# Rows for a decoder trunk's second norm: transposes of y, partly ahead of the up projection, and x added per token

## What is computed

```python
y = jnp.concatenate([o_da, o_gla], axis=-1) @ w_out[l]
h_res = h_res + rmsnorm(y, post_mix_g[l])
h = rmsnorm(h_res, pre_ffn_g[l])
y = conv_ffn(h, w_up[l], conv_w[l], conv_b[l], w_down[l])
h_res = h_res + rmsnorm(y, post_ffn_g[l])
```

## Time and profile before

| | us |
|---|---|
| Median of three runs | 1216.88 |
| Lowest and highest | 1216.7, 1217.07 |
| Profiled execution | 1216.32 |
| Its span | 1214.5 |
| Busy: PE, DVE, ACT, POOL | 1201.5, 663.1, 604.6, 479.8 |

### The profile page before, as it was taken

The page is one execution under the profiler, slowest core; times in us unless marked ns, Lnnn a source line. Parts: engine busy times, 40 slices in busy tenths (PEclk is TensorE's granted clock), DMA queues, the critical chain, the costliest instruction groups (busy, mean ns, idle before and its releaser), DMA issues.

```text
span 1214.5 us, 23728 instructions
## 1 busy us (share of the span) xinstructions
PE 1201.5 (99%) x8948; PEld 1143.9 (94%) x8948; DVE 663.1 (55%) x963; ACT 604.6 (50%) x906; POOL 479.8 (40%) x221
## 2 busy tenths in 40 slices
PE   9999999999999999999999999999999999999997
PEld 8999999999999999999999999999999988888885
DVE  7765545554564346766666666666656743232234
ACT  7544445455674447544445445444444544444444
POOL 1233333323424433444444444444444444444443
PEclk9999999999999999999999999999999999999999
DMA  9655554544436645556565565565655565655641
GB/s 344 188 162 152 150 163 140 146 134 130 148 124 203 192 158 167 171 183 189 174 189 175 176 186 176 186 190 169 193 178 169 192 202 186 198 191 189 200 163 70
DMA packets 172751, 212.31 MB, mean 175 GB/s; under 512 B 6688, under 2 KB 158624, under 8 KB 172576
## 3 DMA queue, kind: packets, MB, share of 16 engines
q1 hardware_dynamic: 172272, 210.32, 55.9%
q10 hardware_dynamic: 432, 1.34, 0.3%
HBM read 209.53 MB, written 2.10 MB: 174 GB/s over the span
## 4 chain that ended last, share of the span: by engine, by line
PE 93%; DVE 3%; ACT 2%; issue 1%; DMA 1%; SPq 0%; DVEq 0%; ACTq 0%
PE psum L416 68%; PE psum L1779 19%; PE psum L1649 1%; PE psum L1419 1%; DVE a_lo L1249 1%; DVE w_lo L400 1%; ACT w_hi L396 1%; DMA raw<-in_w_first 1%; PE psum L1479 1%; PE psum L1807 0%; PE psum L1505 0%; DVE psum L1257 0%; DVE xT L1265 0%; PE psum L1588 0%; PE psum L1606 0%
## 5 line engine op out<-in xcount | busy, mean ns | idle before, releaser
L400 POOL TENSOR_TENSOR w_lo<-raw,w_hi 128x1024 fp32r<-128x1024 f32 x188 | 464.2, 2469 | 707.2 <-ACT w_hi L396 707.2
L416 PE MATMUL psum<-a_hi,w_hi 128*128 128x258 f32 (+1 forms) x2360 | 675.0, 286 | 0.9 <-ACT temp L596 0.8
L416 PE MATMUL psum<-a_lo,w_hi 128*128 128x258 f32 (+1 forms) x2360 | 673.8, 286 | 0.0
L416 PE MATMUL psum<-a_hi,w_lo 128*128 128x258 f32 (+1 forms) x2360 | 670.1, 284 | 0.0
L396 ACT ACTIVATE w_hi<-raw 128x1024 fp32r<-128x1024 f32 x391 | 411.4, 1059 | 470.7 <-PE psum L416 341.5
L400 DVE TENSOR_TENSOR w_lo<-raw,w_hi 128x1024 fp32r<-128x1024 f32 x204 | 269.0, 1320 | 412.0 <-ACT w_hi L396 411.0
L416 PEld LDWEIGHTS psum<-a_hi,w_hi 128*128 128x128 f32 x2360 | 448.3, 190 | 6.6 <-issue 4.3
L416 PEld LDWEIGHTS psum<-a_lo,w_hi 128*128 128x128 f32 x2360 | 448.5, 190 | 0.0
L416 PEld LDWEIGHTS psum<-a_hi,w_lo 128*128 128x128 f32 x2360 | 446.1, 189 | 0.1
L1309 DVE SCALAR_TENSOR_TENSOR proj<-proj,par 128x256 f32<-128x256 f32 x88 | 111.6, 1269 | 38.3 <-ACT proj L812 38.3
L1779 PE MATMUL psum<-w_hi,a_lo 128*128 128x512 f32 x336 | 130.7, 389 | 0.0
(11 more groups left out here) (234 smaller groups left out, 607.8 us busy)
## 6 DMA issues: line engine op xcount, KB each, us to landing
raw<-in_w_up SPq DMA_DIRECT2D x176, 512.0 KB, 3.6
raw<-in_w_in SPq DMA_DIRECT2D x88, 512.0 KB, 4.1
raw<-in_w_down SPq DMA_DIRECT2D x88, 512.0 KB, 4.0
raw<-in_w_out SPq DMA_DIRECT2D x32, 512.0 KB, 3.6
raw<-in_w_first SPq DMA_DIRECT2D x7, 512.0 KB, 10.4
xT<-in_features SPq DMA_DIRECT2D x3, 544.0 KB, 7.2
temp<-in_post_ffn_g ACTq DMA_DIRECT2D x1, 1024.0 KB, 4.7
out<-proj SPq DMA_DIRECT2D x2, 512.0 KB, 2.7
```

The source lines that it names most:

```text
L400: eng.tensor_tensor(w_lo[:, j % SPLIT, :], raw[:, j, :], w_hi[:, j % SPLIT, :], ALU.subtract)\
L416: mm = pe.matmul(psum[:, bank + m, 0:t1 - t0], w[:, j % SPLIT, cols], a[:, k, t0:t1], start=(k == 0 and step == 0), stop=(k == KT - 1 and ...
```

## The change

The transposes for the rows with tokens on partitions are now those of y (`y_T`), not of the sum. They need nothing of the first norm, so groups 0 to 3 stand ahead of the up projection, in banks 5, 0, 1 and 7 and in place of the eight products of constants; the up projection waits until groups 0 to 2 have been copied, VectorE's scaling until group 0 has been. Groups 4 to 7 follow chunks 2 to 5. ScalarE only copies a group. What was missing in it is made per token: x in its natural form (`x_nat`, two loads of 128x2048 on ScalarE's queue from a new input) is added on VectorE, four times 128x1024 (`add_rows`: y times its factor, plus x), and ScalarE squares each result with a sum (`natural_square`). The tokens are grouped so that the first norm's factors lie by token as well: two halo tokens apart, then 2 x 128.

Orders changed with it: ScalarE's split of chunk 3 and the load of the last gain go behind the second scaled tile; VectorE splits chunk 2 right behind the reciprocal, and chunk 3, which was GpSimd's, where it split chunk 2; its first `up_lo` goes ahead of the scaling of tiles 2 and 3; the second norm's row is spread behind chunk 10, not 9, and the splits of chunk 12 go behind the roots and the reciprocals.

The core of the diff:

```diff
-        GROUPS = ((0, P), (P, 2 * P), (NQ - P, NQ))
+        GROUPS = (NM, NM + P, 0)
         SUMS = 260
-        def nat_bank(n):
-            return ROW_BANK if n == 7 else NAT_BANK
+        NAT_BANKS = (Y2_BANK + 1, 0, 1, NAT_BANK, NAT_BANK, NAT_BANK, NAT_BANK, NAT_BANK)
...
+            def load_rows(t):
+                act_e.dma_start(x_nat[:, t, :], x_rows[t * P:(t + 1) * P, :]).then_inc(x_nat_landed, 16)
...
+            def natural(n):
+                act_e.wait_ge(nat_full, n + 1)
+                copy(x1_nat[:, n % 2, (n // 2) * BANK:(n // 2 + 1) * BANK], psum[:, NAT_BANKS[n], :]).then_inc(nat_free, 1)
+
+            def natural_square(t, h):
+                act_e.wait_ge(nat_added, 2 * h + t + 1)
+                act_e.activation(x_nat[:, t, h * CHUNK:(h + 1) * CHUNK], x1_nat[:, t, h * CHUNK:(h + 1) * CHUNK], ACT.Square,
+                                 accum_out=x1_ss[:, t, h:h + 1]).then_inc(nat_squared, 1)
...
+            dve.wait_ge(nat_free, 1)
             for k in range(2):
                 scale_y(k, k + 1, k + 1)
                 add_x(k, k + 1, k + 1)
             for g in range(1, KT // 2):
+                if g == 1:
+                    up_lo(0)
                 scale_y(2 * g, 2 * g + 2, g + 2)
-                up_lo(2 * g - 2)
+                if g > 1:
+                    up_lo(2 * g - 2)
                 add_x(2 * g, 2 * g + 2, g + 2)
                 up_lo(2 * g - 1)
                 if g == 2:
-                    split_lo(dve, OUT1 // RAW, 2)
+                    dve.wait_ge(lo_ready_p, (OUT1 + 2) // 2)
+                    split_lo(dve, OUT1 // RAW, 3)
...
+            def add_rows(t, h):
+                dve.wait_ge(nat_free, 4 * h + 4)
+                dve.wait_ge(x_nat_landed, 32)
+                x1 = x1_nat[:, t, h * CHUNK:(h + 1) * CHUNK]
+                dve.scalar_tensor_tensor(out=x1, in0=x1, scalar=y_rstd[:, t:t + 1],
+                                         in1=x_nat[:, t, h * CHUNK:(h + 1) * CHUNK], op0=ALU.mult, op1=ALU.add)\
+                    .then_inc(nat_added, 1)
...
-            busy(Y2_BANK, 2)
+            natural(0)
+            natural(1, 0, 2)
             pe.wait_ge(y_rstd_made, 1)
...
-            busy(NAT_BANK, 6)
+            natural(1, 2, 4)
+            natural(2)
+            natural(3)
...
             pe.wait_ge(tiles_evacuated, N_BEFORE_UP)
+            pe.wait_ge(nat_free, 3)
...
-                natural(j - 1)
-            natural(7)
-            pe.wait_ge(nat_free, 7)
+                if j < 6:
+                    pe.wait_ge(nat_free, j + 2)
+                    natural(j + 2)
+            pe.wait_ge(nat_free, 8)
```

More of the change, by code:

```diff
@@ L574, in _ @@
                         split_lo(pool, i + (IN1 + j + STREAM_LEAD) // RAW, (j + STREAM_LEAD) % RAW)
+            for c in range(OUT1 - RAW + STREAM_LEAD, OUT1 + STREAM_LEAD - 2):
+                if not lo_on_vector(c):
+                    split_lo(pool, c // RAW, c % RAW)
+            pool.wait_ge(lo_ready_p, (OUT1 + STREAM_LEAD) // 2)
             with pool.Fori(0, N_UP) as i:
@@ L772, in _ @@
                 out_half(i, 1)
+            load_rows(1)
             out_half(N_OUT - 1, 0)
@@ L840, in _ @@
             split_ahead_up(0, 0)
[L841 to L845, removed]
+            for k in range(6, 10):
+                up_hi(k)
             split_ahead_up(0, 1)
-            natural(1)
+            natural(4)
             up_hi(10)
@@ L1434, in spread @@
                 rows = rstd.shape[0]
-                last = cols.stop - cols.start
-                return pe.matmul(psum[:, bank, cols], rstd.broadcast_to([rows, P]), ident[0:rows, rows - last:rows],
+                return pe.matmul(psum[:, bank, cols], rstd.broadcast_to([rows, P]), ident[0:rows, 0:cols.stop - cols.start],
                                  start=True, stop=True)
@@ L1696, in token_sums, with natural @@
             def token_sums(n, squares):
-                for c, (a, b) in enumerate(GROUPS):
-                    mm = pe.matmul(psum[:, ROW_BANK, SUMS + c:SUMS + c + 1], squares[:, a:b], ones[:, 0:1],
-                                   start=(n == 0 and c == 0), stop=(n == 1 and c == 2))
-                return mm
+                for c in (2, 0, 1):
+                    rows = NM if n == 1 and c == 2 else P
+                    a = GROUPS[c]
+                    mm = pe.matmul(psum[0:rows, ROW_BANK, SUMS + c:SUMS + c + 1], squares[:, a:a + rows], ones[:, 0:1],
+                                   start=(n == 0 and c == 2), stop=(n == 1 and c == 1))
+                return mm
+            def natural(n, a=0, b=4):
+                t0 = NM + (n % 2) * P
+                mm = transposes(NAT_BANKS[n], [(kk * P, y_T[:, 4 * (n // 2) + kk, t0:t0 + P]) for kk in range(a, b)])
+                if b == 4:
+                    mm.then_inc(nat_full, 1)
+            for kk in range(4):
+                mm = product(2, RAW - 1, kk, 0, KT - 4 + kk, NQ)
+            mm.then_inc(y_half_made, 1)
+            for kk in range(4):
+                mm = product(3, RAW - 1, kk, 1, KT - 4 + kk, NQ)
+            mm.then_inc(chunk_used, 1)
             pe.wait_ge(y_summed, 2 + KT // 2)
@@ L1718, in up_chunk @@
                 project_chunk(pe, i + OUT1 // RAW, j, bank or 2 * (j // 4), 0, NQ)
[L1720 to L1724, removed]
-                transposes(nat_bank(n), [(kk * P, xT[:, 4 * (n // 2) + kk, t0:t0 + P]) for kk in range(4)])\
-                    .then_inc(nat_full, 1)
             pe.wait_ge(tiles_evacuated, N_BEFORE_UP)
+            pe.wait_ge(nat_free, 3)
             for j in range(2):
```

66 lines of the change are left out of this document (34 added, 32 removed).

## The result

| | before | after |
|---|---|---|
| Median, us | 1217.13 | 1219.20 |
| Profiled execution | 1216.32 | 1218.96 |
| Its span | 1214.5 | 1217.2 |
| Chunk 0 starts | 449.62 | 449.94 |
| Up projection ends | 966.44 | 969.23 |

The changed kernel takes 1.0018 times as long, with a 95% interval of 1.0012 to 1.0025. That is 2.07 us, just inside the 0.2% (2.4 us) that the prediction called the least that can be told from no change, and on the slow side of it. 1219.9 had been forecast. In the profiled executions the difference is 2.64 us. The medians of before and after are those of their common comparison, 19 executions of each.

A forecast was written before the change was run, and what follows sets the result against it. It took TensorE's issue times to bound the kernel. Terms -2.74 + 0.6 + 0.1 + 0.8 + 1.15 + 1.8 + 1.3 gave +3.0 us, 1219.3 for the profiled execution, and with 0.56 for the median 1219.9; range 1214.5 to 1221.3.

The forecast's parts named there:

- The likeliest case: GpSimd first at chunk 5, first add held, two late holds: 1219.9 us, range 1218.7 to 1220.9, chance 0.50.
- Part 1: Transposes ahead of the up projection: chunk 0 0.2 to 0.3 us late but hidden, gross gain 2.74 us by chunk 8.
- part 2: Moved copies let GpSimd go first at chunk 5: +0.6 us in chunk 4, +0.1 at group 7.
- the rival by which the copies hold it up: Ahead of chunk 0, which wants banks 0 and 1, TensorE still waits for copies: up to 0.5 us; no separate chance.
- The rival in which VectorE goes first: At chunk 5 VectorE precedes GpSimd as before, group 7 waits 2.2 us: +4.1, 1221.0 us; chance 0.12.
- Part 3: Adds held by GpSimd, squares waiting, splits of chunks 10 and 11 queued behind: about -0.1 us left at chunk 11.
- The terms +0.8 and +1.15: TensorE's waits in us: 0.8 for the second norm's row, then 1.15 for chunk 11's split.
- Part 4: VectorE copies the row 3.1 us late and meets two more holds: chunk 16 waits +1.8 us, chunk 20 +1.3.
- the 0.3 for "latencies": At chunk 20, the waits' own latencies, included in its forecast wait of +1.3 us.
- Part 5: Two added 1 MB loads on ScalarE's queue: hidden, 0, at most 0.3 us for one issue.
- No late collisions: At chunks 16 and 20 slack covers the late copy, or only one hold hits: 1216.8 to 1218.9 us; chance 0.22.
- The adds pass: First add precedes GpSimd's split of chunk 9 or isn't held by it: faster, 1214.2 to 1214.9 us; chance 0.12.

The follow-up runs named there:

- The first experiment: The changed kernel with ScalarE's split of chunk 10 moved ahead of the first two squares; median -0.06 us against before, ratio 0.9999.
- the late splits: The changed kernel with GpSimd's splits of chunks 17 and 21 made by VectorE; median +0.55 us against before, ratio 1.0004.

## Why the prediction was right, point by point

**Right in mechanism, and high in the sum.** The likeliest case came, with each of its waits at its place, near the low edge of its 1218.7 to 1220.9. The time of 1219.20 is 0.7 us from the forecast, the difference to before (+2.07 for +3.0) is 0.9 us from it: the median taken for before, 1216.88 from three executions, came out as 1217.13, and that helped. The prediction gave 0.56 to "slower", above 1219.3, and 0.34 to "same"; 1219.20 falls on the side of "same", by 0.1 us.

Its sum was +3.0; from the squares' sums to the end of the up projection the profiles give 521.63 us before and 524.20 after, +2.57, and the medians +2.07. Against the sums, chunk 8 is 2.16 us earlier (476.86 - 445.03 = 31.83, before 33.99), and -2.16 + 0.54 + 1.03 + 1.88 + 1.18 = +2.47; the last 0.1 isn't placed.

- *Part 1.* Forecast: both alike at 459.80, chunk 0 0.2 to 0.3 late and that hidden, gross gain 2.74. Measured: 460.01 less the 0.22 of this execution; chunk 0 0.10 late against the sums. From there to chunk 8 it is 16.85 us, before 19.00; with the 0.58 and 0.12 of part 2 taken out, the gross gain is 2.85. Ahead of chunk 0 TensorE stands 1.00 us, 0.51 before, and chunk 0 is only 0.10 later against the sums: the rival by which the copies hold it up is worth no more than that.
- *Part 2.* GpSimd started 0.07 us ahead (460.80, 460.87) and went first, as forecast; tile 8 was held to 463.47 against 463.3. Chunk 4 lasts from 463.79 to 467.26, 3.47 us for 2.89 (+0.58, forecast 0.6), and group 7 comes 0.12 late, behind the copy of group 6 that ends at 470.65 (0.1). Net, chunk 8 is 2.16 earlier where 2.0 was forecast. The rival in which VectorE goes first is out for this execution. But less than the text had is needed to turn the collision round. It named the move of a copy; the kernel with the loads alone shows it turned in the old order as well, with chunk 5 0.61 later. So the 0.6 was sized rightly, and that it counts against before at all may be luck of the one execution that was profiled.
- *Part 3.* (This execution is 0.22 late, so each time is that much earlier against the forecast than it looks.) First add held, to 476.7 (476.5); squares from 476.78 after 3.75 us (3.7); chunk 10's split at 479.03 (478.9); chunk 11's at 484.81 (484.8); GpSimd to 488.3 (488.3). The terms +0.8 and +1.15 came out as 0.54 and 1.03. The first is 0.26 short, one half of it on TensorE's side and one on the row's. With the 0.22 taken out, TensorE stood there at 485.72, not 485.6, and the row was ready for it at 486.26, not 486.4. TensorE needs 0.33 us more than the three chunks counted, for a product of the halo's sum behind chunk 8 (the row at 479.96) that puts chunk 9 at 480.08; chunk 8 itself was 0.16 earlier than forecast. The product was in the kernel before as well. The first experiment shows that these waits come from the order on ScalarE.
- *Part 4.* Row copied at 489.30, or 489.08 with the 0.22 taken out (489.2); chunk 16 +1.88 (+1.8), chunk 20 +1.18 (+1.3), at 517.58 (517.5). The split of the cause wasn't seen, though. The text laid these waits to the row's 3.1 us of lateness. The run without adds has a row only 0.7 late and still waits 0.84 and 1.34, since TensorE's own 2 us are taken from the same reserve of 3.4 and 3.3 us. Either of the two, an early TensorE or a late row, together with the hold of 2.1 us, uses it up. And of the +1.3 the text's own working gives 1.0 (517.5 less 516.5); the 0.3 for "latencies" has no row behind it. The measured 1.18 lies between.
- *Part 5.* Loads at nothing: shown by the run with them alone.
- *The rivals.* "No late collisions" would have given 1216.8 to 1218.9; two held steps of 2.6 us rule it out. Its time and the measured one are only 0.3 us apart, so the median alone would not have told them apart. "The adds pass" is out by the first add: GpSimd, at 473.10, was 0.22 us ahead.

The 0.7 us between forecast and median is 0.3 in the profiled execution (1219.3 against 1218.96). The rest is that the median after lies 0.24 above its profiled execution, where 0.56 had been taken from before. Medians and stretches differ as well, +2.07 and +2.47 for the change. In eight of the nine rows of the table the stretch lies above the median, by 0.30 to 0.69 us. That is what a profile of before that is some 0.3 us short would do, and this one is: its 1216.32 us lies below all but one of the 19 executions of before, and it shows the shorter of the two ways at chunk 5. How many executions of before, if any, go the longer way no run shows, and the rest of the scatter stays open.

## What to carry to other kernels

Before adding work to an engine, ask what is queued behind the instructions that will wait for it: here two exchanged lines on ScalarE were worth 2.1 us, and the added work itself no more than the comparison can resolve (0.2 to 0.3 by the medians). A gain at one stage is real only if the engines behind keep the pace; the stretch that TensorE won was given back two iterations later, by holds that had been hidden in 3.4 us of reserve. When two engines exclude each other, it can be cheaper to give the work to the faster one (1.2 us on VectorE) than to have it held for 2.1 us beside the slower.

## What the runs showed of the hardware

- Which engine is held depends on about a hundredth of a microsecond. GpSimd ahead by 0.02 (461.00, 461.02 with the loads alone; 461.25, 461.27 with the late splits), 0.05 (513.04, 513.09), 0.06 and 0.07 us went first, each time; ahead by 0.01 us (460.66, 460.67) it was VectorE that went first, and that is a single row.
- A held operation doesn't begin anew when GpSimd is done. It ends 0.27 to 0.29 us later if it takes 0.48 alone, and 1.09 later if it takes 1.22 (chunk 12's split, 489.37, against GpSimd's 488.28), so 0.1 to 0.2 us of it are over by then.
- The hold depends on operands and not on the kind of operation: tensor-tensor and scalar-tensor-tensor, of 256, 258 or 1024 elements per partition, were all held with two from SBUF; the 1024-wide add with one in PSUM was not, and GpSimd's split beside it took 2.58 us, as beside the held one (2.55).
